# GpSimd instead of VectorE multiplies the scan's query into its level decays

## The reference, cut to what matters

```python
def gla_chunk_scan(q, k, v, logf, s0):
    # S_t = diag(f_t) S_{t-1} + k_t^T v_t ; o_t = q_t S_t, in chunks
    def step(s, xs):
        bcum = jnp.cumsum(fc, axis=1)
        o_inter = jnp.einsum('bthk,bhkv->bthv', qf * jnp.exp(bcum), s)
        diff = bcum[:, :, None] - bcum[:, None, :]
        decay = jnp.exp(jnp.where(incl[None, :, :, None, None], diff, -jnp.inf))
        att = jnp.einsum('bthk,bshk,btshk->bhts', qf, kf, decay)
        o_intra = jnp.einsum('bhts,bshv->bthv', att, vf)
        ...
```

## Time and profile before

| what | before |
|---|---|
| median of three executions | 3385.09 us |
| the profiled execution's own time | 3387.63 us |
| its span in the trace | 3385.8 us |
| mixers and mix of layer 0 / layer 1 | 2080 to 2740 us / 2740 to 3386 us |

### The profile page before, as it was taken

How to read it: one execution, slowest core, us unless ns; L and a number is a source line. 1 busy time by engine, 2 the same in 40 slices (tenths; PEclk the granted TensorE clock), 3 DMA queues, 4 the chain that set the end, 5 groups by cost and what they waited for, 6 DMA issues and landing times.

```text
span 3385.8 us, 55096 instructions
## 1 busy us (share of the span) xinstructions
PE 3175.8 (94%) x20656; PEld 2402.2 (71%) x20656; DVE 1430.8 (42%) x2928; ACT 1155.6 (34%) x1978; POOL 1407.4 (42%) x2232
## 2 busy tenths in 40 slices
PE   8999999999999999999999999888989888789888
PEld 6888777787787786777687787765666667556555
DVE  3222554222532225444422225564464345554644
ACT  3222333122422223111322225444444335445544
POOL 4555564454554454333255454441342224233323
PEclk9999999999999999999999999989989999889989
DMA  4222222323323332111123332100100212001011
GB/s 149 94 99 93 87 87 81 140 100 136 107 104 136 124 112 75 57 63 57 56 100 136 126 114 102 33 27 20 39 27 21 75 44 75 26 26 38 33 47 61
DMA packets 74360, 264.76 MB, mean 78 GB/s; under 512 B 7856, under 2 KB 9136, under 8 KB 73904
## 3 DMA queue, kind: packets, MB, share of 16 engines
q1 hardware_dynamic: 69584, 246.02, 20.4%
q10 hardware_dynamic: 4576, 15.98, 1.3%
HBM read 252.53 MB, written 7.34 MB: 77 GB/s over the span
## 4 chain that ended last, share of the span: by engine, by line
PE 82%; DVE 10%; ACT 4%; issue 3%; POOL 1%; DMA 0%; DVEq 0%; ACTq 0%; SPq 0%; POOLq 0%
PE ps L1455 28%; PE ps L1484 18%; PE ps L1460 14%; PE ps L1448 3%; PE ps L1983 3%; PE ps L1956 2%; PE ps L2006 2%; PE ps L1558 1%; DVE tb L2666 1%; PE ps L1850 1%; PE ps L1789 1%; PE ps L2036 1%; DVE tb L2300 1%; PE ps L1539 1%; ACT tb L1349 1%
## 5 line engine op out<-in xcount | busy, mean ns | idle before, releaser
L950 POOL TENSOR_TENSOR wl<-raw,wh 128x256 fp32r<-128x256 f32 x1640 | 1212.9, 772 | 1757.3 <-ACT wh L1054 1134.7
L1076 ACT ACTIVATE wh<-raw 128x1024 fp32r<-128x1024 f32 x224 | 237.9, 1062 | 976.0 <-PE ps L1460 833.5
L1455 PE MATMUL ps<-xh,wh 128*128 128x512 f32 x1392 | 542.4, 390 | 2.0 <-ACT pr L1155 2.0
L1455 PE MATMUL ps<-xl,wh 128*128 128x512 f32 x1392 | 541.6, 389 | 0.0
L1460 PE MATMUL ps<-xh,wl 128*128 128x512 f32 x1392 | 344.2, 389 | 1.6 <-POOL wl L950 1.6
L1054 ACT ACTIVATE wh<-raw 128x1024 fp32r<-128x1024 f32 x186 | 196.9, 1059 | 428.6 <-PE ps L1484 248.5
L1455 PEld LDWEIGHTS ps<-xh,wh 128*128 128x128 f32 x1392 | 261.3, 188 | 59.6 <-issue 5.0
L1460 PEld LDWEIGHTS ps<-xh,wl 128*128 128x128 f32 x1392 | 261.1, 188 | 56.9 <-POOL wl L950 2.9
L1455 PEld LDWEIGHTS ps<-xl,wh 128*128 128x128 f32 x1392 | 261.4, 188 | 53.9
L1455 PE MATMUL ps<-ah,wh 128*128 128x512 f32 x748 | 296.2, 396 | 0.8 <-DVE al L2287 0.8
L1455 PE MATMUL ps<-al,wh 128*128 128x512 f32 x748 | 291.6, 390 | 0.0
(11 more groups left out here) (372 smaller groups left out, 4890.5 us busy)
## 6 DMA issues: line engine op xcount, KB each, us to landing
raw<-wts_dram SPq DMA_DIRECT2D x458, 512.0 KB, 3.5
spilled_dram<-hc ACTq DMA_DIRECT2D x1, 3072.0 KB, 8.7
hc<-spilled_dram ACTq DMA_DIRECT2D x1, 3072.0 KB, 11.7
tb<-tab_dram ACTq DMA_DIRECT2D x5, 512.0 KB, 3.6
spilled_dram<-hc ACTq DMA_DIRECT2D x1, 2048.0 KB, 7.6
hc<-spilled_dram ACTq DMA_DIRECT2D x1, 2048.0 KB, 8.6
out_dram<-hc SPq DMA_DIRECT2D x8, 256.0 KB, 2.1
hc<-x_dram SPq DMA_DIRECT2D x7, 256.0 KB, 6.7
```

What stands on the lines that cost most here:

```text
L950: ins = pool.tensor_tensor(wl[:, n % SPLIT, piece], raw[:, LOADED[n] % RAW, piece], wh[:, n % SPLIT, piece].bitcast(F32), ALU.subtract)
L1076: act.activation(wh[:, n % SPLIT, :], raw[:, at % RAW, :], ACT.Copy).then_inc(hi_done, 1)
L1455: pe.matmul(out_, wh[:, s, k * P:(k + 1) * P], x_(k, at), start=first, stop=False)
```

## The change

The function `operands` moves, word for word, from the VectorE program to the GpSimd program, and GpSimd's walk of the step list calls it where the list has `operands`. Its eight multiplications, their operands and both its waits (`q_silu`, `decay_ready`) and its signal (`ops_ready`) are as before.

```diff
@@ GpSimd
+            def operands(w, p):
+
+                layer, hp, way, s, t, full, n = scan_of(w, p)
+                if p == 0:
+                    pool.wait_ge(q_silu, 2 * layer + hp + 1)
+                pool.wait_ge(decay_ready, s + 1)
+                if not full:
+                    pool.sem_inc(ops_ready, 1)
+                    return
+                ins = pool.tensor_tensor(qi[s % 2], qi[s % 2], sq_q[:, t * P:(t + 1) * P], ALU.mult)
+                for l in range(LEVELS):
+                    z, q_ = halves(level(s, l), l)[1 - way], halves(sq_q[:, t * P:(t + 1) * P], l)[1 - way]
+                    ins = pool.tensor_tensor(z, z, q_, ALU.mult)
+                ins.then_inc(ops_ready, 1)
+
             def mixers(layer):
                 for step, *at in mixer_steps(layer):
                     if step == "dist":
                         dist(*at)
+                    elif step == "operands":
+                        operands(*at)
                     elif step == "round":
@@ VectorE
-            def operands(w, p):
-                ...
-                ins = dve.tensor_tensor(qi[s % 2], qi[s % 2], sq_q[:, t * P:(t + 1) * P], ALU.mult)
-                for l in range(LEVELS):
-                    z, q_ = halves(level(s, l), l)[1 - way], halves(sq_q[:, t * P:(t + 1) * P], l)[1 - way]
-                    ins = dve.tensor_tensor(z, z, q_, ALU.mult)
-                ins.then_inc(ops_ready, 1)
-
```

More of the change, by code:

```diff
@@ L2741, in mixed @@
                     split(t, ahk(y, TOK)[:, 0:n_q], alk(y, TOK)[:, 0:n_q], a_ready, "a")
-                run_ = dict(quarter=quarter, finish=finish, rope=lambda f: rope(f[1], f[0]), scores=scores, shift=shift, math=math_, keep=keep, end=end, y=mixed, table_in=table, operands=operands, take=take, update=update,
+                run_ = dict(quarter=quarter, finish=finish, rope=lambda f: rope(f[1], f[0]), scores=scores, shift=shift, math=math_, keep=keep, end=end, y=mixed, table_in=table, take=take, update=update,
                             sums=sums, rms=lambda hp: scan_rms(layer, hp), turn=lambda hp: turn(layer, hp), out=lambda hp: scan_end(layer, hp))
```

## The result

The changed kernel takes 3397.63 us (median of eight, 3393.47 to 3401.53), the kernel before 3380.40 on the same chip (eight, 3377.3 to 3388.61). The ratio of the two, taken from the means of the runs, is 1.0047, with 95% between 1.0038 and 1.0055: it is slower by 13 to 19 us. I had forecast 3386 and "within 0.3%" as the likeliest; it is slower by more than that.

The account below looks back on a forecast made before the run. TensorE, busy 94% of the span, was taken as the bound. Places +1.9, VectorE's other work -2.5 and engines in each other's way +1.5 gave +0.9 us, so about 3386 us for the median; range 3373 to 3400.

Parts of the forecast that it names:

- three kinds of place: Step's place in GpSimd's queue: no differences ahead, products waiting; differences and perhaps a remainder ahead, products waiting; slack (25 of 40).
- (0,5): Position with no differences ahead on GpSimd: step done before VectorE's update, products start 1.2 us sooner.
- (7,2): Position with the next differences ahead on GpSimd: products 2.1 us later, the worst.
- (4,4): Position with differences and a remainder ahead on GpSimd: products 0.7 us later, listed as 0.8.
- (1,1) and (3,0): Positions read as late: products 1.3 us later at the first; at the second, slack turns late, +1.4.
- (4,2) and (7,4): Positions where TensorE was idle before the products: these start 1.3 and 1.6 us later.
- terms for the products alone: Starts of TensorE's products: later places +8.1 us, sooner places -5.2, one slack place turned late +1.4.
- -2.5 us for VectorE's other work: Next VectorE instruction can start 1.25 us earlier; a quarter of eight such positions, between 0 and -10 us.
- blocking: GpSimd's added work stretches VectorE operations with two SBUF inputs by 5 us; partly off the path, +1.5, between 0 and +5.
- GpSimd becomes the link: Slower rival: step of 3.1 us +7, full blocking +3.5, clock +6; in sum +17.5, 3403 us; chance 0.22 beyond 10 us.
- Hidden gain: Faster rival: VectorE's 64.9 us count for more than the chain shows; 3367 us; chance 0.18 beyond 10 us.
- the chain's 18: Step's pieces at 12 of 40 positions on the chain of waits: 18 us given back if the step cost nothing.

Follow-up runs that it names:

- late_nine: Kernel before with the step on GpSimd only at the nine positions read as late, on VectorE at the other 31; 3401.7 us, ratio 1.0058.
- none_vector: Kernel before with the eight multiplications left out, VectorE still waiting and signalling; 3363.33 us, ratio 0.9939.
- none_gpsimd: Changed kernel with the eight multiplications left out, GpSimd still waiting and signalling from its queue; 3369.65 us, ratio 0.9966.
- fives: Step on GpSimd only at the eight positions p = 5, on VectorE at the other 32; 3382.51 us, ratio 0.9996.
- mixed: Changed kernel with the step back on VectorE at the nine positions read as late, on GpSimd at the other 31; 3380.13 us, ratio 0.9998.
- late_long: Changed kernel with the multiplications replaced by three waves of eight GpSimd memsets (2.39 us) before the signal; 3390.9 us, ratio 1.0028.
- round_behind: Changed kernel with a weight tile's remainder between decay and step done behind the step on GpSimd; 3394.18 us, ratio 1.0034.
- changed, again: Changed kernel run once more, unaltered, for a second trace; 3394.82 us, ratio 1.0044 of the kernel before.
- shadow: Kernel before plus eight unneeded GpSimd multiplications of the same shapes where the changed kernel has the step, nobody waiting; 3401.05 us, ratio 1.0049.
- operands_first: Changed kernel with GpSimd doing the step ahead of the next position's differences, not behind them; 3406.88 us, ratio 1.0072.

## Why the prediction was right and wrong

**Right: the bound, the step's length, most of the places.** TensorE stayed the bound; GpSimd's largest wait is still for ACT's rounded tiles, 611.4 us. The step takes 2.46 us for my 2.3, inside the bounds. That is 1.98 times VectorE's 1.24, as the Trainium skill has it (GPSIMD Engine Reference, 4.1 Engine selection: about twice as slow with two inputs). All three kinds of place were seen: (0,5) 1.0 us sooner for 1.2, (7,2) 1.85 later for 2.1, (4,4) 1.4 for 0.8. At (1,1) and (3,0), 1.3 and 1.4 forecast, the two traces of the changed kernel differ: 1.0 and 2.0 at the first, 2.0 and 1.4 at the second. Two late places missed: (4,2) and (7,4) moved by 0.1 us each, for 1.3 and 1.6. In `late_nine` they moved by 1.3 and 1.6 to 1.8, so the reading of the queue held there and something else in the changed kernel took it up. Directly before the products the idle time rose by 4.1 us. The forecast's terms for the products alone, 8.1 - 5.2 + 1.4, make 4.3, and that they agree so well is partly luck, since the misses offset each other. The whole idle time moved by -1.1 us where the sum had +0.9. As a forecast of idle time the sum was right, though no run isolates its -2.5 us for VectorE's other work.

**Wrong: the step from idle time to time.** The sum ended at +0.9 us because it priced each wait by its length and took TensorE's own work as fixed. Its clock stood only in the rival, as 6 us, tied to a step of 3.1 us ("decides from the point where the step on GpSimd passes about 2.8 us"). With 2.46 us and no more idle time, TensorE's busy time grew by 12 us. The idle time is the same in sum but lies in longer pieces: of 2 us or more, without the one at the end of the span, there are 16 in both traces of before (53.2 and 53.3 us) and 21 in both of the changed kernel (64.8 and 65.0). The 2 us are where I chose to count, not a level at which anything was seen to switch. On this reading, moving 1 us from (0,5) to (7,2) is not neutral: the places that got shorter had 1.85 us at most, and (1,3), (3,0), (4,4) and (7,2) have 2.0 to 3.5 now.

The sum needed two terms, then: the idle time, and what the clock takes. Both can be read for every kernel. The idle term is the idle time of its trace less the 147.3 us of before. The clock term is the drop of the mean granted clock over all its runs, against before on the same chip, times 3383 us.

| | effect | idle term | clock term | both | mean clock | idle pieces of 2 us or more |
|---|---|---|---|---|---|---|
| `none_vector` | -20.6 | -12.3 | -12.7 | -25.0 | 0.9722 | 15 |
| `none_gpsimd` | -11.5 | -10.1 | -2.5 | -12.6 | 0.9692 | 17 |
| `fives` | -1.4 | -5.4 | -0.1 | -5.5 | 0.9687 | 16 |
| `mixed` | -0.7 | -9.0 | +2.5 | -6.5 | 0.9677 | 17 |
| `late_long` | +9.5 | +5.4 | +4.8 | +10.2 | 0.9673 | 22 |
| `round_behind` | +11.5 | -1.9 | +11.5 | +9.6 | 0.9653 | 22 |
| changed, again | +14.9 | -1.1 | +11.1 | +10.0 | 0.9652 | 21 |
| `shadow` | +16.6 | +9.1 | +8.4 | +17.5 | 0.9660 | 21 |
| `late_nine` | +19.6 | +6.8 | +15.2 | +22.0 | 0.9642 | 20 |
| `operands_first` | +24.4 | +7.3 | +16.4 | +23.7 | 0.9636 | 23 |

The two terms together follow the measured effect to within 6 us, over a range of 45. For the change itself the idle term is -1.1 and the clock term 11 to 13. The pieces of idle time go with the clock, but loosely. Before has 16 of them at a mean clock of 0.9685 to 0.9687; all kernels that lose have 20 or more, those that don't have 17 or fewer, yet `late_long` with 22 lost little clock. This is a correlation, not a proof. What exactly makes the clock drop, none of these kernels isolates.

**Wrong: my test for it.** I wrote that a PEclk within 0.01 in both stages would mean "right". It was (0.95 to 0.94, 0.92 to 0.92), and proves nothing: one hundredth of some 1306 us is 13 us, nearly the whole effect. And the one trace that I had was on the low side of its own kernel, 0.967 where the next shows 0.971. Another sign failed as well: VectorE's busy time was to fall by 65 to 75 us, and fell by 49.4.

**Wrong in size: blocking.** I expected 5 us of stretching for VectorE's other work from the moved multiplications. VectorE's busy time holds about 15 more (64.9 out, 49.4 gone), of which 8 to 10 come with the multiplications and the rest is unexplained. Most of it is covered: reads and blocking together cost about 5 us of time where I had 1.5, though with an interval from none to 11. The Trainium skill (SBUF — State Buffer, SBUF: two separate sides) says that the loser of the shared port pair is held for the whole instruction of the other. Here that is too little: the L2674 at (4,4) was held over three groups of GpSimd instructions, for 3.06 us, and in `shadow` a multiplication over the rest of four subtractions and all of eight multiplications, for 4.77.

**The rivals.** "GpSimd becomes the link" came nearer to the result (3403 against 3397.63) than the forecast of 3386, through its clock term and not through the long step that it was tied to: of its 17.5 us, 7 were for a step of 3.1 us that never came, and its clock term of 6 us was about half of what the clock took. I gave it 0.22. That my range reached to 3400 was owed to this rival. "Hidden gain" falls as it stands. Taking the step off VectorE does give back 20.6 us, the chain's 18 within the interval, but that is spent again, 9 us on the queue and 26 on the work.

**What stays open.** That the 15 us lie in the clock rests on two traces of each kernel and on the mean clock of the runs. That the clock fell because of the longer waits is argued from (7,2) and from the table, not isolated. What the 5 to 7 us of extra VectorE time are that come without the multiplications, no run shows.

## What to carry to other kernels

Before moving a step to an idle engine, write down for each of its instances what stands ahead of it in the new queue and who waits for it: nine instances of forty made the whole loss here, and the other 31 together moved for nothing. A bound engine's waits are not paid by their sum alone; a wait made longer where one already was can cost the clock behind it, so count the long pieces of idle time as well as the total. And look at a second trace of the unchanged kernel before trusting a difference of a few tenths of a per cent, since two executions of the same kernel, at a granted clock of 0.967 and 0.971, were 9 us apart here.

## What the runs showed of the hardware

- One VectorE instruction with two SBUF inputs can be held over many GpSimd instructions in a row, not over one: 160 ns of work took 3.06 us at (4,4) of the changed kernel, 0.29 us took 4.77 at (1,1) of `shadow`, each ending within 0.15 us of GpSimd's run.
- GpSimd's multiplications of 128x64 last 308 to 367 ns but start 0.28 us apart, so a step of eight is 2.46 us, with a spread of only 0.05 over the 40 of the first trace; the same step on VectorE varied from 1.24 to 3.3 us. GpSimd isn't always the steady one: in the second trace of the changed kernel one step, at (1,1), took 3.45 us, with a multiplication of 862 ns in it.
- The same program showed 195.4 and 225.3 us at half clock in two executions, and the span followed: 3377.0 and 3385.8.
